# Expert loop with seven weight buffers instead of six, two instead of four for gathered rows, another pass order, and a last stage without GpSimd

## What is computed

```python
h = silu(x @ w1[e]) * (x @ w3[e])        # per expert e, w1 and w3 1024 x 256
h = h * gate[:, e]                       # two nonzero gates per token
y = y + h @ w2[e]                        # w2 256 x 1024
out = rms_norm(x_residual + y, final_norm_g)
```

## Time and profile before

| | us |
|---|---|
| median of 3 runs | 1565.28 (1562.81 to 1565.93) |
| profiled execution | 1564.52 |
| its span, first to last instruction | 1562.7 |
| router block, DVE's first to last instruction | 1091.9 to 1135.5 |
| expert loop on PE | 1149.9 to 1498.1 |
| last stage, DVE's first instruction to the end | 1514.6 to 1562.7 |

### The profile page before, as it was taken

One profiled execution on the slowest core, in us unless ns is written; L12 is line 12 of the kernel. 1 busy time (PEld: TensorE's weight loads), 2 busy tenths in 40 slices (PEclk: granted clock), 3 DMA queues, 4 the chain that ended last, 5 costly groups with the idle time before them and its releaser, 6 DMA issues. The chain is left out here.

```text
span 1562.7 us, 32324 instructions
## 1 busy us (share of the span) xinstructions
PE 1302.4 (83%) x13762; PEld 995.7 (64%) x13762; DVE 663.3 (42%) x1362; ACT 425.1 (27%) x870; POOL 503.4 (32%) x423
## 2 busy tenths in 40 slices
PE   7898879999999999999999997786249979688730
PEld 6787669889889889889889876575223423233210
DVE  2659543444344354354355345452812212121137
ACT  2152223234234234234233223221012211111124
POOL 1515451371372272272263264220011111111016
PEclk9999879999999999999999998796569989899875
DMA  9958238737736836836835814801946998998955
GB/s 268 258 163 263 64 112 241 220 97 232 230 97 204 257 97 195 267 97 191 271 97 166 256 37 140 85 18 37 355 166 208 319 372 294 361 346 292 335 203 214
DMA packets 276440, 317.40 MB, mean 203 GB/s; under 512 B 17724, under 2 KB 255880, under 8 KB 274992
## 3 DMA queue, kind: packets, MB, share of 16 engines
q1 hardware_dynamic: 262232, 275.77, 57.1%
q0 software_dynamic: 8272, 22.85, 3.9%
q10 hardware_dynamic: 5792, 16.70, 3.5%
HBM read 295.94 MB, written 27.68 MB: 207 GB/s over the span
## 5 line engine op out<-in xcount | busy, mean ns | idle before, releaser
L1477 PE MATMUL psum<-arena 128*128 128x256 f32 (+3 forms) x1536 | 314.2, 359 | 3.2 <-DMA arena<-in_w_in 3.2
L1477 PEld LDWEIGHTS psum<-arena 128*128 128x128 f32 x1536 | 259.9, 196 | 33.9 <-DMA arena<-in_w_in 3.4
L2309 PE MATMUL psum<-arena 128*64 128x512 f32 (+1 forms) x832 | 181.0, 632 | 48.5 <-DMA arena<-in_exp_w 48.5
L2309 PEld LDWEIGHTS psum<-arena 128*64 128x64 f32 (+1 forms) x832 | 57.8, 140 | 154.2 <-issue 151.4
L1189 DVE COPY_PREDICATED arena<-arena,psum 128x128 f32<-128x128 int32 x280 | 84.9, 303 | 144.0 <-PE psum L1660 137.1
L1473 PE MATMUL psum<-arena 128*128 128x128 f32 x1152 | 138.2, 280 | 4.3 <-DVE arena L1057 4.3
L640 POOL TENSOR_TENSOR arena<-arena 128x768 f32<-128x768 f32 (+1 forms) x32 | 59.0, 1845 | 250.1 <-ACT arena L850 250.1
L1473 PEld LDWEIGHTS psum<-arena 128*128 128x128 f32 x1152 | 133.6, 195 | 6.9 <-issue 6.4
L1435 PE MATMUL psum<-arena 64*64 64x64 f32 x3264 | 119.8, 226 | 15.1 <-ACT arena L861 10.5
L1435 PEld LDWEIGHTS psum<-arena 64*64 64x64 f32 x3264 | 107.7, 139 | 33.1 <-issue 14.9
L1739 PE MATMUL psum<-arena 128*128 128x256 f32 x512 | 117.4, 388 | 0.8 <-ACT arena L932 0.8
(11 more groups left out here) (416 smaller groups left out, 2017.6 us busy)
## 6 DMA issues: line engine op xcount, KB each, us to landing
arena<-in_w_in SPq DMA_DIRECT2D x96, 1024.0 KB, 6.6
arena<-in_exp_w SPq DMA_DIRECT2D x96, 1024.0 KB, 12.5
arena<-in_w_out SPq DMA_DIRECT2D x32, 1024.0 KB, 6.0
arena<-in_w_in SPq DMA_DIRECT2D x24, 512.0 KB, 5.4
arena<-y_d SPq DMA_DIRECT2D x8, 1024.0 KB, 12.0
arena<-in_x_prompt ACTq DMA_DIRECT2D x15, 512.0 KB, 4.3
arena<-in_w_in SPq DMA_DIRECT2D x8, 576.0 KB, 5.2
out<-arena POOLq DMA_DIRECT2D x9, 512.0 KB, 3.0
```

Source lines behind the costliest of these rows:

```text
L1477: ins = mm(b[:, 0:n], hT[:, c, :], w[:, c, 0:n], start=(c == 0), stop=(c == KC - 1))
L2309: ins = mm(bank[2 + q % 2][at:at + width, :], xT[q % 2][:, c, at:at + width], w13[n % NB][:, c, :], start=(c == 0), stop=(c == KC - 1))
```

## The change

Seven weight buffers instead of six, paid for by two instead of four buffers each for gathered rows (X), results (Y) and index columns, by h1, sg and h in a part of the constants that only the mixer reads, and by the router's scratch and fg in weight buffer 6. The semaphore of a weight buffer is split: w1 and w3 are loaded anew once mm1 of the last quad is done, w2 once mm2 is done; mm1 waits for w1 and w3 only, mm2 for w2. SP no longer loads positions 4 and 5 in the router block; it loads them in the loop's block after the first two gathers have landed. The order of the passes is another. In the last stage DVE does scale and gain in one operation after the sums of the next tile, ACT issues the stores, and POOL does nothing. fg is loaded with the x2 rows of position 27.

```diff
-TS, NB, AT_ONCE, PACK = 32, 6, 4, 4096
+TS, NB, AT_ONCE, PACK = 32, 7, 4, 4096
-SEQUENCE = "HHHLHLMLHLMLHL"
+SEQUENCE = "HHHMLHLHLMLHLL"
...
-    NX = 4
+    NX = 2
...
-    h1, sg, h, hT = take(256), take(256), take(256), [take(256) for _ in range(2)]
+    h1, sg, h = (const[:, C_LV + 256 * n:C_LV + 256 * n + 256] for n in range(3))
+    hT = [take(256) for _ in range(2)]
...
-    x2 = [w2[2 + t // 2][:, t % 2, :] for t in range(NT)] + [w2[0][:, 0, :]]
+    x2 = [w2[(N_EXP - NB + t // 2) % NB][:, t % 2, :] for t in range(NT)] + [w2[1][:, 0, :]]
...
+    tot = [flat[4][:, 2 * D:3 * D], flat[4][:, 3 * D:4 * D], flat[5][:, 3 * D:4 * D]]
+    fg = flat[6][:, 0:D]
...
     def load_ranked(sp, n):
 
         hold(sp)
         e = sp.value_load(by_rank[0:1, RANK_OF[n]:RANK_OF[n] + 1], min_val=0, max_val=N_EXP - 1)
-        load_from(sp, e, n % NB, weights_in(n % NB))
+        if n >= NB:
+            sp.wait_ge(step("mm1"), LAST_QUAD[n - NB] + 1)
+        load_13(sp, e, n % NB, w13_in(n % NB))
+        if n >= NB:
+            sp.wait_ge(step("mm2"), LAST_QUAD[n - NB] + 1)
+        load_2(sp, e, n % NB, w2_in(n % NB))
...
             for e in range(AT_ONCE):
-                load_w(sp, e, e, weights_in(e))
-            sp.wait_ge(step("by_rank"), 1)
-            for n in range(AT_ONCE, NB):
-                load_ranked(sp, n)
+                load_w(sp, e, e)
...
-            for n in range(NB, N_EXP):
-                sp.wait_ge(step("mm2"), LAST_QUAD[n - NB] + 1)
+            for u in range(2):
+                sp.wait_ge(step(f"xg_in{u}"), 16)
+            for n in range(AT_ONCE, N_EXP):
                 load_ranked(sp, n)
-            for n in range(N_EXP - NB, N_EXP - 2):
+            for n in range(N_EXP - NB, N_EXP - NB + 4):
                 sp.wait_ge(step("mm2"), LAST_QUAD[n] + 1)
                 for t in (2 * (n - N_EXP + NB), 2 * (n - N_EXP + NB) + 1):
                     sp.dma_start(x2[t], x2_d[t * P:t * P + P, :]).then_inc(step(f"x2_in{t}"), 16)
-            sp.dma_start(fg, A["final_norm_g"].partition_broadcast(P)).then_inc(step("fg_in"), 16)
+                if n % NB == 6:
+                    sp.dma_start(fg, A["final_norm_g"].partition_broadcast(P)).then_inc(step("fg_in"), 16)
...
                 for at, width, n in QUADS[q]:
-                    pe.wait_ge(weights_in(n % NB), 48 * (n // NB + 1))
+                    pe.wait_ge(w13_in(n % NB), 32 * (n // NB + 1))
...
                 after(pe, "y_b", q, 2)
+                for at, width, n in QUADS[q]:
+                    pe.wait_ge(w2_in(n % NB), 16 * (n // NB + 1))
...
-        @block.gpsimd
-        def _(pool):
-            for n, t in enumerate(sequence):
-                u, R = n % 3, slice(0, count[t])
-                pool.wait_ge(step("f_scaled"), n + 1)
-                nc.gpsimd.tensor_tensor(fo[u][R, :], fo[u][R, :], fg[R, :], ALU.mult).then_inc(step("f_out"), 1)
-                pool.wait_ge(step("f_out"), n + 1)
-                pool.dma_start(out[rows[t], :] if t < NT else out_s, fo[u][R, :]).then_inc(step(f"f_stored{u}"), 16)
...
-                act.wait_ge(step("f_rs"), 3 * n + 3)
-                if n >= 3:
-                    act.wait_ge(step(f"f_stored{u}"), 16 * (n // 3))
-                a(fo[u][R, :], Y[u][R, :], ACT.Copy, scale=st[:, 2:3]).then_inc(step("f_scaled"), 1)
+                if n:
+                    store(n - 1)
+            store(NTT - 1)
...
+            def normed(n):
+                t = sequence[n]
+                u, R = n % 3, slice(0, count[t])
+                dve.wait_ge(step("f_rs"), 3 * n + 3)
+                if n >= 3:
+                    dve.wait_ge(step(f"f_stored{u}"), 16 * (n // 3))
+                v.scalar_tensor_tensor(fo[u][R, :], tot[u][R, :], fs[R, 4 * n + 2:4 * n + 3], fg[R, :],
+                                       ALU.mult, ALU.mult).then_inc(step("f_out"), 1)
+
+            dve.wait_ge(step("fg_in"), 16)
+            for n in range(NTT):
+                sums(n)
+                if n:
+                    normed(n - 1)
+            normed(NTT - 1)
```

More of the change, by code:

```diff
@@ L1839, in hold @@
         eng.sem_inc(held[eng.engine], 1)
-    NX = 4
+    NX = 2
     W = KC * 512 + 2 * D
     wall = take(NB * W)
+    assert NB == 7
     w13 = [wall[:, b * W:b * W + KC * 512].rearrange("p (c n) -> p c n", c=KC) for b in range(NB)]
@@ L1859, in experts @@
     fs, eps = take(4 * NTT), take(1)
-    fg_area = take(T2 * 64)
-    fg = fg_area[:, 0:D]
     spare = [0]
@@ L1867, in borrow @@
         spare[0] += n
-        assert spare[0] <= NX * D
-        return Yall[:, spare[0] - n:spare[0]]
+        assert spare[0] <= W
+        return wall[:, 6 * W + spare[0] - n:6 * W + spare[0]]
     slot_hot = borrow(T2 * P)
@@ L1881, in experts @@
     d4, e4, ohg = (borrow(NTT * 4) for _ in range(3))
-    tile_hot = fg_area[:, 0:T2 * 64]
+    tile_hot = borrow(T2 * 64)
     sel, cand = tile_hot[:, 0:NTT * 8], tile_hot[:, NTT * 8:2 * NTT * 8]
@@ L1896, in experts, with load_w @@
     fo = [flat[5][:, D * n:D * n + D] for n in range(3)]
[L1898 to L1901, removed]
+    tot = [flat[4][:, 2 * D:3 * D], flat[4][:, 3 * D:4 * D], flat[5][:, 3 * D:4 * D]]
+    fg = flat[6][:, 0:D]
+    def load_w(eng, e, buf):
+        eng.dma_start(w13[buf][:, :, 0:256], A["exp_w1"][0, e].rearrange("(p c) n -> p c n", c=KC)).then_inc(w13_in(buf), 16)
+        eng.dma_start(w13[buf][:, :, 256:512], A["exp_w3"][0, e].rearrange("(p c) n -> p c n", c=KC)).then_inc(w13_in(buf), 16)
+        eng.dma_start(w2[buf], A["exp_w2"][0, e].rearrange("(c p) n -> p c n", c=2)).then_inc(w2_in(buf), 16)
     def load_ranked(sp, n):
@@ L1906, in load_ranked, with load_13, load_2, w13_in @@
         e = sp.value_load(by_rank[0:1, RANK_OF[n]:RANK_OF[n] + 1], min_val=0, max_val=N_EXP - 1)
-        load_from(sp, e, n % NB, weights_in(n % NB))
-    def load_from(sp, e, buf, sem):
+        if n >= NB:
[4 more added lines that the diff above has]
+        load_2(sp, e, n % NB, w2_in(n % NB))
+    def load_13(sp, e, buf, sem):
         w1v = A["exp_w1"][0].rearrange("e (p c) n -> e p c n", c=KC)
         w3v = A["exp_w3"][0].rearrange("e (p c) n -> e p c n", c=KC)
-        w2v = A["exp_w2"][0].rearrange("e (c p) n -> e p c n", c=2)
         sp.dma_start(w13[buf][:, :, 0:256], w1v[bass.ds(e, 1)]).then_inc(sem, 16)
         sp.dma_start(w13[buf][:, :, 256:512], w3v[bass.ds(e, 1)]).then_inc(sem, 16)
+    def load_2(sp, e, buf, sem):
+        w2v = A["exp_w2"][0].rearrange("e (c p) n -> e p c n", c=2)
         sp.dma_start(w2[buf], w2v[bass.ds(e, 1)]).then_inc(sem, 16)
-    def weights_in(b):
-        return step(f"weights_in{b}")
+    def w13_in(b):
+        return step(f"w13_in{b}")
+    def w2_in(b):
+        return step(f"w2_in{b}")
     def bcast(ap, n, dim=2):
@@ L2355, in body @@
                 e = sp.value_load(ov_exp_i[0:1, bass.ds(i, 1)], min_val=0, max_val=N_EXP - 1)
-                load_from(sp, e, 1, step("o_weights"))
+                load_13(sp, e, 1, step("o_weights"))
+                load_2(sp, e, 1, step("o_weights"))
             further(sp, body)
@@ L2462, in _ @@
                 load_y(t)
-        @block.gpsimd
-        def _(pool):
-            for n, t in enumerate(sequence):
-                u, R = n % 3, slice(0, count[t])
-                pool.wait_ge(step("f_scaled"), n + 1)
-                nc.gpsimd.tensor_tensor(fo[u][R, :], fo[u][R, :], fg[R, :], ALU.mult).then_inc(step("f_out"), 1)
-                pool.wait_ge(step("f_out"), n + 1)
-                pool.dma_start(out[rows[t], :] if t < NT else out_s, fo[u][R, :]).then_inc(step(f"f_stored{u}"), 16)
-            for u in range(3):
-                pool.wait_ge(step(f"f_stored{u}"), 16 * (NTT // 3))
         @block.scalar
@@ L2478, in _, with store @@
             a = nc.scalar.activation
+            def store(n):
+                t = sequence[n]
+                act.wait_ge(step("f_out"), n + 1)
+                act.dma_start(out[rows[t], :] if t < NT else out_s, fo[n % 3][0:count[t], :]).then_inc(step(f"f_stored{n % 3}"), 16)
             for n, t in enumerate(sequence):
@@ L2482, in _ @@
                 act.wait_ge(step("f_sum"), n + 1)
-                a(X[0][R, :], Y[u][R, :], ACT.Square, accum_out=st[:, 0:1]).then_inc(step("f_rs"), 1)
+                a(Y[0][R, :], tot[u][R, :], ACT.Square, accum_out=st[:, 0:1]).then_inc(step("f_rs"), 1)
                 act.wait_ge(step("f_rs"), 3 * n + 1)
@@ L2487, in _ @@
                 a(st[:, 2:3], st[:, 1:2], ACT.Exp, scale=-0.5).then_inc(step("f_rs"), 1)
-                act.wait_ge(step("f_rs"), 3 * n + 3)
-                if n >= 3:
-                    act.wait_ge(step(f"f_stored{u}"), 16 * (n // 3))
-                a(fo[u][R, :], Y[u][R, :], ACT.Copy, scale=st[:, 2:3]).then_inc(step("f_scaled"), 1)
+                if n:
+                    store(n - 1)
+            store(NTT - 1)
+            for u in range(3):
+                act.wait_ge(step(f"f_stored{u}"), 16 * (NTT // 3))
         @block.vector
@@ L2495, in _, with sums @@
```

(14 more changed lines are left out.)

## The result

The changed kernel takes 1508.38 us, median of 4 runs (1507.07 to 1510.55), against 1565.61: a ratio of 0.9639, 95% interval 0.9622 to 0.9656. The forecast was 1519.8 with a range of 1510 to 1532. The profiled execution took 1507.07.

The account below looks back on a forecast made before the run. The expert loop was taken as bound by weight supply. Loop end 1462.3, 16.5 between, 34.3 last stage and 4.9 end gave a 1518.0 span; with 1.8 beyond the span, 1519.8 us, range 1510 to 1532.

Parts of the forecast that it names:

- Bound by supply: Expert loop: weight supply sets the pace; PE's waits near 20 us in 4 pieces, at quads 16, 17, 20 and 23.
- Bytes of the supply: Loop from 1252.0 to the last quad's mm1: 70.2 MB at 368 GB/s, 190.8 us, plus 2 us to land.
- Start of the loop: From router barrier to first transposes: 7.9 us earlier, with 3.8 less at the barrier and the gather landing in 4.4.
- Rival (c): Loop start: no earlier, the gather takes 8.5 for its own reasons; +4.1 us, 1524. Chance 0.06.
- (a): Late release in the loop: SP sits at a w2 wait, so the split gives nothing; 1525 to 1529. Chance 0.12.
- Pass order at nothing: Expert loop: the new order of passes costs nothing, 3 us either way.
- Two buffers at nothing: Expert loop: two buffers for gathered and stored rows cost nothing; the store's cover is 0.8 us up to a landing of 10.0.
- (e): Expert loop: two Y buffers make it slower than before, loop 65 us longer than forecast, 1585. Chance 0.04.
- Behind the loop: From mm2's end to DVE's first last-stage operation: scatter, drain and barriers, 16.5 us kept, a microsecond less possible.
- Last stage: After the loop: 27 DVE operations without POOL, 34.3 us, then 4.9 behind the last multiply; together 8.9 less.
- Rival (d): Last stage: DVE slow from something other than POOL, 10.5 of 27 operations slow; +21 us, 1541. Chance 0.04.
- rival (b): Loop supply slower, at 361 GB/s, more of the stream being w1 and w3 beside indirect traffic: +3.7, 1523.5. Chance 0.07.

Follow-up runs that it names:

- the pairs: Changed kernel, but SP sends w1 and w3 of both experts freed by the same quad, then waits for mm2 and sends both w2: 1500.82 us, ratio 0.9578.
- full rows: Changed kernel, but every gather and scatter moves all 128 rows, empty places reading row p and writing to added rows: 1517.25 us, ratio 0.9684.

## Why the forecast went wrong where it did

**Bound by supply: right.** The four waits lie at quads 16, 17, 20 and 23 as forecast, 14.4 us against some 20. Six buffers, the split undone and the pairs all move the loop the way of the bytes sent ahead: 9.5, 6.6 and 4.2 us, where the bytes alone (3.1, 2.1 and 1.07 MB at 368 GB/s) would be 8.5, 5.7 and 2.9.

**Bytes of the supply: the step that failed.** "An expert is 3.146 MB, a gather or a scatter 0.524 MB", and from it "12 gathers and 14 scatters, 13.6 MB". It was 9.0 MB, since the rows of empty places are not moved. From the release of w2 of expert 13 to the start of the last mm1 the forecast had 192.8 us, and the trace has 184.5: 8.3 of the 9.0 us by which the forecast loop was too long. With the full rows put back the stretch takes 191.6, so the bytes are worth 7.1 us. At the forecast's 368 GB/s the missing 4.6 MB should be 12.5 us. Two terms take some of it back: q1 moved 57.9 MB where 56.6 were counted (3.6 us; w2 of expert 31, six x_d loads and the gains leave before the last mm1 and were not in the sum, though the trace does not show that they are the difference), and the rate was 364 (2.0 us). The 2 us put for the landing are not seen as time of their own, and the slow mm1 put at 2.2 us behind the stretch cost 1.6. The transfer's size could have been had from the page before: 22.85 MB on q0, less 4.23 of stores and 1.70 of the mixer, is 0.352 MB for each of 48 transfers, so 9.2 MB for 26. One small slip in the same passage changes nothing: 1406 + 13.9 + 2 x 11.7 is 1443.3 and not 1443.8.

**Start of the loop: right.** 8.0 us less in place of 7.9, and by both parts of the sum: DVE's idle time at the barrier fell from 4.80 to 0.97, 3.8 as forecast, and the gather takes 4.3 to the transposes where 4.4 was taken. The late loads of 4 and 5 cost all of it again, 9.6 us of start. Rival (c) is out.

**The split: right, (a) is out.** Undone, it costs 6.6 us of loop, where 5.7 to 9 had been put.

**Pass order at nothing: right**, 0 to 1.5 us. **Two buffers at nothing: right**, (e) is out with 0.9988.

**Behind the loop: kept at 16.5, was 14.1.** The text had the cause and only allowed for "a microsecond less": with two x_d loads in front instead of four and the gains, the last scatter lands in 2.8 us instead of 5.0. Six buffers, which put the loads back in front, give 17.9.

**Last stage: right**, 34.1 and 5.0 against 34.3 and 4.9. The stage undone on the changed kernel costs 9.1. Rival (d) is out: no operation is slow without POOL beside it.

**Router: costed at nothing, gained 1.6.** "Smaller memsets ... beside DVE's router chain, nothing" looked for cover and missed that POOL's memsets slow the very chain that is critical. Four memsets restore 43.6.

**Supply rate, rival (b).** The saturated stretch ran at 364, inside the 361 to 375 of the bounds, and at 374 with full rows. So the rate alone went the way of (b), by 2.0 us where (b) had 3.7, and the missing bytes outweighed it. The 358 GB/s of the Trainium skill, "DMA: Bandwidth & Descriptors", section on where 436 GB/s comes from, is not a ceiling here.

**The range.** Its lower end had the rate, one slow mm1 and a microsecond of scatter, but no term for the bytes, which I took as known. That is the term that decided.

## What to carry to other kernels

Before a supply is summed, divide the megabytes that the page shows for a queue by its transfers, with every other DMA of that queue taken off first. The indirect DMAs here moved only the rows in bounds, and the stream with the gaps ran at fewer GB/s (364 against 374), so take both from the trace. With in-order issue, the order of waits in the issuing queue is worth as much as a buffer: seven buffers gave 9.5 us, the split 6.6, and sending the second expert's free parts ahead of the first one's last wait another 4.2 at no memory. Before counting a helper engine's work as hidden, ask whether it slows the engine that it stands beside.

## What was not expected of the hardware

- DVE's operations of 2 to 32 columns took 0.70 to 0.89 us beside POOL's memsets and 0.15 to 0.25 without, and the chain paid 1.6 us for two memsets. In the last stage operations with two inputs in the arena took 3.2 to 3.4 us beside POOL's multiply of 2.4 to 2.9, and 1.27 to 1.28 alone. The Trainium skill, "SBUF — State Buffer", section on who interferes with whom, says that such pairs of instructions exclude each other for their whole length on a shared port pair. These rows agree with it; the runs show the slowing and its end, not the port.
- An empty place still passes as a packet. q0 has 3744 packets in the stretch with and without full rows; the packets under 512 B fall from 2433 to 1301 when the places are filled, and 1132 rows of 4 KB are the 4.6 MB.
- The saturated DMA engines moved 364 GB/s with a third of the indirect places empty and 374 with all of them filled. By the two DMA views (share times length, divided by MB) the packets of q1 took 2.9 us of the 16 engines per MB in both kernels and those of q0 2.5 with full rows, so the bytes added were cheaper than the average. What limits the rate was not tested further.
- POOL's drain at the end of the expert loop takes 3.97 us, before and after the change, and all engines wait for it. No run tries to avoid it.
- A short wait can be followed by a slow mm1 or not: 8.68 us after 2.61 (changed kernel, quad 23), 7.09 after 3.33 (split undone, quad 16). In both the wait before that lies three quads back, so it does not tell them apart. The runs do not settle what decides.
